# The second attention of a two-block transformer kernel: keys as two tiles and values as one, the values turned by transposes, in place of weights padded with zero columns

## What is computed

```python
qkv = h @ w_qkv + b_qkv                       # 1024 -> 16 query heads, 2 key heads, 2 value heads, 64 wide each
q, k, v = split(qkv, [1024, 1152])
scores = einsum(q, band(k)) * 64 ** -0.5 + rel_bias      # each query chunk of 64 sees 192 keys
p = exp(scores - m) / (sum(exp(scores - m)) + exp(sink - m))
out = einsum(p, band(v)) @ w_o + b_o          # 8 query heads share a key head and a value head
x = x + out
```

## Time and profile before

| | before |
|---|---|
| median of 3 runs | 1858.51 us (1858.46 to 1860.97) |
| profiled execution: time | 1860.72 us |
| profiled execution: span of the core | 1858.8 us |
| mean granted TensorE clock | 0.969 |
| TensorE matmul busy | 1732.1 us (93%) |
| VectorE busy | 1464.2 us (79%) |
| ScalarE busy | 1167.8 us (63%) |
| GpSimd busy | 122.7 us (7%) |
| moved from and to HBM | 516.64 MB, mean 278 GB/s |
| weight granules loaded | 456 x 1 MB, median 6.8 us to landing |

### The profile page before, as it was taken

How to read it: one execution, slowest core, us unless ns; L and a number is a source line. 1 busy time by engine, 2 the same in 40 slices (tenths; PEclk the granted TensorE clock), 3 DMA queues, 4 the chain that set the end, 5 groups by cost and what they waited for, 6 DMA issues and landing times.

```text
span 1858.8 us, 26648 instructions
## 1 busy us (share of the span) xinstructions
PE 1732.1 (93%) x10308; PEld 1535.2 (83%) x10308; DVE 1464.2 (79%) x1446; ACT 1167.8 (63%) x1154; POOL 122.7 (7%) x112
## 2 busy tenths in 40 slices
PE   7887899997889999878999999999999999999994
PEld 6777799997889999767888888888888888888883
DVE  7888788866766655655888888888888898888886
ACT  5434467754244444444778778787787877877774
POOL 1000054421020001001000000000000000000000
PEclk9988999998899999898999999999999999999997
DMA  7432378585345556313999999999999999999994
GB/s 294 148 114 91 120 292 355 185 195 204 136 159 182 182 191 232 143 46 138 381 372 362 396 371 380 382 354 402 376 362 402 360 392 365 369 400 364 386 368 167
DMA packets 75598, 516.64 MB, mean 278 GB/s; under 512 B 8000, under 2 KB 8384, under 8 KB 17024
## 3 DMA queue, kind: packets, MB, share of 16 engines
q1 hardware_dynamic: 68976, 489.75, 69.1%
q0 software_dynamic: 6544, 25.81, 4.6%
HBM read 491.41 MB, written 24.12 MB: 277 GB/s over the span
## 4 chain that ended last, share of the span: by engine, by line
PE 80%; DVE 12%; ACT 5%; issue 2%; DMA 1%; POOL 0%; DVEq 0%; POOLq 0%; SPq 0%; ACTq 0%
PE psum L661 25%; PE psum L663 25%; PE psum L662 25%; DVE wlo L1392 4%; ACT whi L1025 3%; DVE acc L1507 2%; PE psum L960 1%; DVE al L1433 1%; PE psum L711 1%; ACT s L1242 0%; DMA par<-params 0%; PE psum L931 0%; DMA yrow<-expert_outs,idx 0%; PE psum L868 0%; POOL ssum L582 0%
## 5 line engine op out<-in xcount | busy, mean ns | idle before, releaser
L1392 DVE TENSOR_TENSOR wlo<-wraw,whi 128x2048 fp32r<-128x2048 f32 x456 | 1043.2, 2291 | 242.5 <-ACT whi L1025 124.3
L1330 ACT ACTIVATE whi<-wraw 128x2048 fp32r<-128x2048 f32 x336 | 643.7, 1918 | 212.0 <-PE psum L663 212.0
L661 PE MATMUL psum<-ah,whi 128*128 128x256 f32 x1176 | 344.3, 293 | 22.1 <-DVE al L1433 12.9
L661 PE MATMUL psum<-whi,xgh 128*128 128x512 f32 x896 | 356.2, 398 | 1.6 <-DVE xgl L1392 1.6
L663 PE MATMUL psum<-whi,xgl 128*128 128x512 f32 x896 | 351.4, 392 | 0.0
L662 PE MATMUL psum<-wlo,xgh 128*128 128x512 f32 x896 | 349.9, 391 | 0.0
L662 PE MATMUL psum<-al,whi 128*128 128x256 f32 x1176 | 337.4, 287 | 0.0
L663 PE MATMUL psum<-ah,wlo 128*128 128x256 f32 x1176 | 337.0, 287 | 0.0
L1025 ACT ACTIVATE whi<-wraw 128x2048 fp32r<-128x2048 f32 x118 | 225.2, 1910 | 150.1 <-PE psum L663 146.4
L661 PEld LDWEIGHTS psum<-ah,whi 128*128 128x128 f32 x1176 | 230.9, 196 | 26.7 <-issue 10.4
L662 PEld LDWEIGHTS psum<-al,whi 128*128 128x128 f32 x1176 | 230.8, 196 | 0.7
(11 more groups left out here) (334 smaller groups left out, 2076.2 us busy)
## 6 DMA issues: line engine op xcount, KB each, us to landing
wraw<-weights SPq DMA_DIRECT2D x456, 1024.0 KB, 6.8
expert_rows<-zeros POOLq DMA_DIRECT2D x1, 8704.0 KB, 43.4
expert_outs<-ysb SPq DMA_DIRECT2D x9, 512.0 KB, 7.8
expert_outs<-zeros POOLq DMA_DIRECT2D x1, 4096.0 KB, 59.5
xgt<-expert_rows SPq DMA_DIRECT2D x8, 512.0 KB, 8.2
bias_rows<-ttab POOLq DMA_DIRECT2D x1, 3072.0 KB, 36.9
btab<-bias_rows POOLq DMA_DIRECT2D x1, 2048.0 KB, 12.8
xres<-x SPq DMA_DIRECT2D x1, 1024.0 KB, 6.9
```

The source lines that it names most:

```text
L661: nc.tensor.matmul(out, lh, rh, start=start, stop=False)
L1330: sc.activation(whi[:, g % NS, :], wraw[:, g % NW, :], ACT.Copy).then_inc(hi_done, 1)
L1392: return ve.tensor_tensor(dst, value, hi.bitcast(f32), SUB)
```

## The change

The padded weight columns go. The two key heads become two tiles that each hold one head twice (64 columns, repeated), and the two value heads one plain tile of 128 columns, computed like the keys, tokens along the row. They are drained into a new tile `kk` (3 x 256), which lies where the score tile `s2` lies later. `k2` and `v2` are zeroed by GpSimd ahead of its two copies into `btab`. ScalarE writes each key head from `kk` to its two tiles in `k2`, the matching 64 partitions each, with the bias; it adds the value bias in `kk`. TensorE turns the values by two transposes behind query jobs 0 to 2, and VectorE copies them from PSUM into the zeroed `v2`, two copies of 128 x 256. The broadcast bias `bv`, its load, and the turning of `rstd` go.

The plan: 2 granules fewer (116 in place of 118 ahead of the experts). Keys take one granule in place of two; values and query 0 share the next one. So queries 1 and 2, 3 and 4, 5 and 6 share a granule now, where it was 0 and 1, 2 and 3, 4 and 5, 6 and 7.

```diff
@@ make_plan
     at["k2"] = len(p.jobs)
     for kv in range(2):
-        for hi in range(2):
-            p.tile("od_w_qkv_2", KD, spread(1024 + kv * 64, 64, 64 * hi, 64 * (1 - hi)))
+        p.tile("od_w_qkv_2", KD, spread(1024 + kv * 64, 64) * 2)
     at["v2"] = len(p.jobs)
-    cols = []
-    for kv in range(2):
-        for hi in range(2):
-            cols += spread(1152 + kv * 64, 64, 64 * hi, 64 * (1 - hi))
-    p.fresh()
-    where = [(*p.put(512, "od_w_qkv_2", k * P, cols), k) for k in range(KD)]
-    p.jobs += [list(where), list(where)]
-    p.fresh()
+    p.tile("od_w_qkv_2", KD, spread(1152, P))
     at["q2"] = len(p.jobs)
@@ program, tiles
-        bv = place("bv", [P, 512], f32, 22 * KB)
+        kk = place("kk", [P, 3, T], f32, 64 * KB)
@@ gpsimd
-            pool.dma_start(bv[:], bv_d).then_inc(late, 16)
...
             wait_job(pool, AT["k2"] - 1)
+            pool.memset(k2[:], 0.0).then_inc(keys_zeroed, 1)
+            pool.memset(v2[:], 0.0).then_inc(keys_zeroed, 1)
@@ tensor
-            for i in range(4):
+            for i in range(2):
                 job(AT["k2"] + i, ah, al, lambda k: (h_lo, 4 * KD + k + 1))
                 if i == 0:
                     summed_squares(6)
-            def turn_rstd(count):
-                pe.wait_ge(rstd_done, count)
+            job(AT["v2"], ah, al)
+            def turn_values():
+                pe.wait_ge(value_biased, 1)
                 for t in range(2):
-                    mm = nc.tensor.transpose(bank[7][:, t * P:(t + 1) * P], rstd[:, t * P:(t + 1) * P], ident)
-                mm.then_inc(rtm_mm, 1)
-            turn_rstd(1)
-            while PIECES[at_piece[0]][0] < AT["q2"]:
-                piece(at_piece[0], ah, al, None, moving=PIECES[at_piece[0]][0] - AT["v2"])
-                at_piece[0] += 1
+                    mm = nc.tensor.transpose(bank[7][:, t * P:(t + 1) * P], kk[:, 2, t * P:(t + 1) * P], ident)
+                mm.then_inc(values_turned, 1)
...
             for p in range(3):
                 job(AT["q2"] + p, ah, al)
+            turn_values()
             scores2(0)
@@ scalar
-            for i in range(4):
-                n = AT["k2"] + i
+            act.wait_ge(keys_zeroed, 1)
+            for kv in range(2):
+                n = AT["k2"] + kv
                 split_past(n)
                 wait_drained(act, n)
-                sc.activation(k2[:, i, :], k2[:, i, :], ACT.Identity, bias=pcol("bk", i)).then_inc(key_biased, 1)
-            split_to(last_granule(AT["v2"]) - 1)
-            split_to(last_granule(AT["v2"]))
+                for a in range(2):
+                    h = slice(64 * a, 64 * a + 64)
+                    sc.activation(k2[h, 2 * kv + a, :], kk[h, kv, :], ACT.Identity,
+                                  bias=par[h, COL["bk"] + kv:COL["bk"] + kv + 1]).then_inc(key_biased, 1)
+            n = AT["v2"]
+            split_past(n)
+            wait_drained(act, n)
+            sc.activation(kk[:, 2, :], kk[:, 2, :], ACT.Identity, bias=pcol("bv", 0)).then_inc(value_biased, 1)
@@ vector
-            for i in range(4):
-                split_to(last_granule(AT["k2"] + i))
-                drain(AT["k2"] + i, k2[:, i, :])
-                split_past(AT["k2"] + i)
-            token_rstd(1)
-            split_to(last_granule(AT["v2"]) - 1)
-            split_to(last_granule(AT["v2"]))
-            for t in range(2):
-                m = AT["v2"] + t
-                wait_job(v, m)
-                ve.scalar_tensor_tensor(v2[:, t, :], bank[m % 4][:, :], rtm[:, t:t + 1], bv[:], MUL, ADD
-                                        ).then_inc(drained[m % 4], 1)
+            for i in range(3):
+                n = AT["k2"] + i
+                split_to(last_granule(n))
+                drain(n, kk[:, i, :])
+                split_past(n)
+            def values():
+                v.wait_ge(keys_zeroed, 2)
+                v.wait_ge(values_turned, 1)
+                for a in range(2):
+                    dst = v2[:, :, :].rearrange("p t (kv c) -> p t kv c", kv=2)[:, :, :, 192 * a:192 * a + 64]
+                    ve.tensor_copy(dst, bank[7][:, 0:T].rearrange("p (t kv j) -> p t kv j", t=2, kv=2))
...
             query(0)
             query(1)
+            values()
             before_exp(0)
```

More of the change, by code:

```diff
@@ L206, in pieces @@
             mine = [x for x in tiles if x[0] == g]
-            if n == AT["v2"]:
-                out.append([n, mine, g == gs[-1], False])
-                out.append([n + 1, mine, g == gs[-1], True])
-            else:
-                out.append([n, mine, g == gs[-1], False])
+            out.append([n, mine, g == gs[-1], False])
     last = {}
@@ L480, in program @@
         max_done = sem("max_done")
-        key_biased, query_biased, rtm_ready = sem("key_biased"), sem("query_biased"), sem("rtm_ready")
+        keys_zeroed, key_biased, query_biased = sem("keys_zeroed"), sem("key_biased"), sem("query_biased")
+        value_biased = sem("value_biased")
         tr_done, pt_done, pv_done = sem("tr_done"), sem("pt_done"), sem("pv_done")
@@ L1728, in _ @@
                 link(ve.tensor_tensor(zc[:, i, :], zc[:, i, :], rstd[:], MUL))
-            v.wait_ge(late, 48)
+            v.wait_ge(late, 32)
             for i in range(4):
@@ L2022, in pack_params @@
     bqkv = a["od_b_qkv_2"][0]
-    bk = np.zeros((2, 2, 2, 64), np.float32)
-    for kv in range(2):
-        for hi in range(2):
-            bk[kv, hi, hi] = bqkv[1024 + kv * 64:1024 + (kv + 1) * 64]
+    bk = np.stack([bqkv[1024 + kv * 64:1088 + kv * 64] for kv in (0, 0, 1, 1)])
     parts = {n: columns(a[n]) for n, _ in PARAMS if n in a}
@@ L2029, in pack_params @@
     parts["bk"] = columns(bk.reshape(-1))
+    parts["bv"] = columns(bqkv[1152:1280])
     parts["router"] = a["od_router_2"][0].reshape(KD, P, NE).transpose(1, 0, 2).reshape(P, KD * NE)
@@ L2071 @@
                               "od_w_qkv_2", "od_w_o_2", "od_exp_gate_2", "od_exp_up_2", "od_exp_down_2")}
-    bv = a["od_b_qkv_2"][0, 1152:]
-    bvp = np.zeros((2, 2, 2, 64), np.float32)
-    for kv in range(2):
-        for hi in range(2):
-            bvp[kv, hi, hi] = bv[kv * 64:(kv + 1) * 64]
     arrays = {
```

21 lines of the change are left out of this document (6 added, 15 removed).

## The result

Four runs of the changed kernel have a median of 1871.29 us (1868.74 to 1873.34), beside 1859.47 for the kernel before on the same chip. The ratio is 1.0062, 95% interval 1.0045 to 1.008: **0.6% slower**, where 1854.5 us was forecast, in a range from 1851.0 to 1859.0.

A forecast was written before the change was run, and what follows sets the result against it. It took matmuls to bound most stages, but the wait for GpSimd's second bias copy to bound the changed place. First scores 6.0 us earlier and a loop 2.0 longer gave 1858.51 - 4.0 = 1854.5 us, range 1851.0 to 1859.0.

The forecast's parts named there:

- The load of `bv` and the narrower parameter table: Loads hundreds of us before the changed place: hidden under matmuls, so nothing gained or lost.
- all of it shifts: Everything behind the attention loop: keeps its order and only moves in time with the earlier end of the loop.
- My own test: Expert loop: a length differing from before by over 1 us would show the prediction wrong.
- First scores, -6.0: Start of the loop over pairs: first scores at 756.6 in place of 762.63, 6.0 us earlier.
- The memset held by the split: GpSimd's second memset falls behind VectorE's split at 731: 2.2 us later, total 1856.7; chance 0.27, including another case.
- The loop, +2.0: Loop over pairs: four rounds with a split in place of three, 55.8 us against 53.8, 2.0 us later.
- my first rival: Loop: both rounds without a split at full clock, 6.82 us each; total gain 5.9 us, 1852.6 us; chance 0.22.
- the forecast's case: Loop: of two rounds without a split, one takes 6.82 us and one 8.74; total 1854.5 us; chance 0.34.
- The slower rival: Loop: TensorE at 1.2 GHz throughout, 12.9 us over now, less 6.0; total 1865.4 us; chance 0.08.
- The experts swallow it: Expert stage: weight transfers run ahead all along, so earlier compute gains nothing, 1858.5 us; chance 0.06.
- TensorE as the path: Keys, values and queries ahead of the loop: the whole 14.2 us saved on TensorE come, 1844.3 us; chance 0.03.
- The sum: Whole kernel: -6.0 at the first scores plus 2.0 in the loop, -4.0 us, giving 1854.5 us.

The follow-up runs named there:

- e1_gap: Changed kernel plus an unused 64-byte tile behind the parameter tile, so later tiles keep their addresses from before the change: 1857.14 us, ratio 0.999 to the kernel before.
- e5_ah_up: Changed kernel with 64 unused bytes ahead of `ah` and `al` instead of behind the parameters: 1854.97 us, ratio 0.9985 to the kernel before.
- e6_all_up: Changed kernel with 64 unused bytes ahead of `whi`, moving weights' halves, `ah`, `al` and the region up together: 1875.24 us, ratio 1.0093 to the kernel before.
- e9_experts_up: Changed kernel with only the experts' operand tiles, and the tiles behind them, 64 bytes higher: 1859.78 us, ratio 1.0009 to the kernel before.
- e11_both: Changed kernel, 64 unused bytes behind parameters, bias copies before memsets, query drains and value copies before masks, experts' operands 64 bytes higher: 1842.82 us, ratio 0.991.
- e3_wall: Changed kernel with two unused granules appended to the weight array, restoring its earlier size in HBM: 1872.84 us, ratio 1.0083 to the kernel before.
- e2_before_low: Kernel before, with the flag tile moved into the parameter tile's padding so the region's tiles lie 64 bytes lower: 1877.08 us, ratio 1.0107.

## Why the prediction was wrong, point by point

- **The step that failed** is the one that priced the parameter table: "The load of `bv` and the narrower parameter table lie hundreds of us earlier, under matmuls", at nothing. I costed its load, and not the addresses behind it. It moved operands of 528 + 4032 matmuls from r = 192 to 128 and cost 2.8 + 14.1 = 17 us in the traces. By the medians it is 14.2 us (1871.29 against 1857.14; 13 by the ratios 1.0062 and 0.999), and 18.7 where the kernel before got the same shift (1877.08 against 1858.39). With it fell the sentence on what comes behind the loop, "all of it shifts". My own test, an expert stage whose length differs by over 1 us, was the one that spoke.
- **First scores, -6.0.** From the last sum it was -6.7 in the changed kernel and -5.45 in `e1_gap`. GpSimd's last sum starts 4.28 us later than before and the second copy is issued 6.05 later: the memsets cost 1.77, forecast 1.90. It landed after 15.2 for 16.3 us (16.4 in `e1_gap`); that scatter is most of the difference. VectorE waited 6.19 us for the bias, forecast some 7.
- **The memset held by the split** did not come. The second ran from 735.35 beside a split from 735.55: 0.96 and 2.29 us, both unstretched, where the add took 2.13. The Trainium skill (SBUF — State Buffer, section Who interferes with whom) states the rule more narrowly than the page that the prediction cites: a VectorE instruction with two SBUF inputs contends with a GpSimd instruction that reads SBUF, not with one that only writes it. The one add and the one memset that the traces have beside a split agree: the add reads, the memset does not.
- **The loop, +2.0**, was mis-sized: +0.17. Round 0 took 10.33 (forecast 10.4), but both free rounds 6.81 and 6.82 at clock 1.00, my first rival. In `e5_ah_up`, `e6_all_up`, `e9_experts_up` and `e11_both` one took 8.7 or 8.8, so the forecast's case does occur.
- **The slower rival**, TensorE at half clock through the loop, had the right sign and the wrong mechanism: the loop's clock was 0.87, and the loss lay elsewhere.
- **The experts swallow it** did not come either: in `e1_gap` the last sum of `w_o` is 5.67 us earlier than before, the experts take 998.43 us for 998.46, and all of it reaches the end of the trace. **TensorE as the path** fell with the wait for the bias, 6.19 us on VectorE.
- **The sum.** With the addresses held, change against no change is 1857.14 against 1858.39 at the old distances, and 1872.84 (`e3_wall`) against 1877.08 (`e2_before_low`) at the new: -1.3 and -4.2, forecast -4.0. The first is short of the forecast by more than half. The traces show about 5 us gained at the place (-5.45 + 0.17 in `e1_gap`); why the median of `e1_gap` keeps only a part of it is open, since its ten runs differ among themselves by up to 6.5 us. Two things vary by such amounts in the traces, the clock behind the loop (3.7 us) and the second pace (2 us for a down projection); which of them the runs without a trace met is not shown.

## What to carry to other kernels

When a change resizes, adds or drops a tile, list the addresses of every matmul's two operands before and after, not only the instructions: a tile that nobody waits for can move all that lies behind it. When a stage that the change does not touch changes its length at the same clock and count, compare the time from start to start of single matmuls first, and put the addresses back with an unused tile before judging the change. Then look for what varies by itself, here the pace behind a pause and the clock behind the loop, before giving a difference of 2 to 4 us between two traces to the change. Where a long stage streams through TensorE, a few placements of its operands are worth measuring on their own.

## What the runs showed of the hardware

- TensorE's pace in these fp32r matmuls depends on the distance of the two operands in SBUF, with a period of 256 bytes: for 24 of 128x256 from 2.83 to 2.99 us (6%), for 24 of 128x512 from 5.56 to 5.72 (3%), with nothing else running. These are times of blocks with the small matmul at their end. Of the steps of 64 bytes the best differs by shape: 192 for the first, 0 for the second; in steps of 16 bytes single blocks at 144 and 16 were a little shorter still (2.83 and 5.56).
- Clock (1.00 in all these windows) and busy share show nothing of it: the slow down projection is as busy as the fast one. Only the time from start to start does.
- At the distance 192 a stream of 128x256 matmuls has two steady paces, 0.113 and 0.118 us from start to start, at equal addresses and clock 1.00. In `e1_gap` it changed from one to the other in the middle of a stage, at a wait of TensorE for `fl`. What decides between them was not found.
- The stretch from the last scores to the last sum of `w_o` takes 37.9 us or up to 42.2 with the same work, by the clock granted in its first 18 us (0.91 or 0.64).
